# Down products of the feed-forward layers in seven block products, with sums by way of DRAM and the low parts of activation blocks on GpSimd

## The chip, the cores and the metric

The kernel runs on one core of one Trainium2 chip. The metric is the device time of one execution in microseconds; a kernel's time is the median of its runs.

## The reference

One inference step of a one-layer encoder with 1024 prompt tokens and 8 x 16 sample tokens, model width 1024. A feed-forward layer stands at each end of the layer, and both are what matters here (width of the hidden layer 2816):

```python
def swiglu(x, w_gate, w_up, w_down):
    return (jax.nn.silu(x @ w_gate) * (x @ w_up)) @ w_down

x = x + 0.5 * swiglu(rms_norm(x, w['ffn1_norm']), w['ffn1_w_gate'], w['ffn1_w_up'], w['ffn1_w_down'])
# sparse attention and a gated delta rule in parallel, merged, projected and added to x
x = x + 0.5 * swiglu(rms_norm(x, w['ffn2_norm']), w['ffn2_w_gate'], w['ffn2_w_up'], w['ffn2_w_down'])
y = rms_norm(x, final_norm)
```

Everything is float32.

## The kernel before

All 1152 tokens lie in nine tiles of 128 (`x`, one tile to a row of 1024). Each float32 operand of a matrix product is split in a high part, rounded to the type that TensorE takes, and a low part, the rest; `three_passes` (line 151) makes a product as high x high, high x low, low x high. ScalarE writes the high part with a copy, VectorE (in a few places GpSimd) the low part with a subtraction.

`ffn` (line 398) runs twice. Its *gate and up* stage goes over 22 units: unit 2n is the gate weights of a pair n of hidden tiles, unit 2n + 1 the up weights. Six of the nine token tiles are already multiplied there in seven block products, with sums of weight blocks (`take_sum`) and of token blocks; the three plain tiles (`PLAIN`) are multiplied as they are. The items of a unit (`EIGHT`, `SEVEN` in the first four units) pass through a ring of six (`ring`): `keep_item` on ScalarE, `rest_item` on VectorE, `half_item` on TensorE; VectorE folds partial results (`folds`, line 859), ScalarE takes the silu, VectorE the product with the up half (line 850), and SyncE stores the pair's activations to DRAM (`act_d`, line 502).

The *down* stage reads them back by k-tiles: 22 in the second layer, 20 in the first, whose last two are left to the next stage (`Pending`). SyncE loads an activation tile and a weight tile (`load_slot`, lines 512 and 513), two in flight, ScalarE copies the high parts (lines 700 and 702), VectorE makes the low parts (lines 906 and 908), seven slots hold them. `groups` divides the k-tiles in seven groups; for each group TensorE makes all 18 outputs of 128 tokens x 512 columns (`down_proj`, line 1104), three products to a k-tile, and VectorE adds each to `x` (`add_down`, line 920). In the last group of the second layer a tile's final norm follows its two additions (`finish_tile`, line 923; squares on ScalarE, line 580), and SyncE stores it (line 566).

GpSimd makes low parts of the first four items and of the sums of tokens (lines 1004 and 1011) and does nothing more in the layer. Each engine runs its instructions in the order of the code; semaphores order the engines. The profile's tile names carry `ffn_` for both layers.

## Time and profile before

| | us |
|---|---|
| median of 3 runs | 2903.29 |
| lowest, highest | 2898.73, 2906.71 |
| the profiled execution | 2895.88 |
| its span, first to last instruction | 2894.1 |

Busy shares of the span: TensorE 95%, its weight loads 89%, VectorE 60%, ScalarE 35%, GpSimd 15%. The DMA engines moved 247.85 MB. The two feed-forward layers take the first 789 us and the last 830 us or so of the span; what lies between is attention, the delta rule and the merge. In the rows, PE is TensorE, DVE is VectorE, ACT is ScalarE, POOL is GpSimd and SP is SyncE; `SPq` and `POOLq` are DMA issues of these; L840 is line 840. Busy time counts overlapping products once.

### The profile page before, as it was taken

How to read it: one execution, taken by the hardware profiler on the slowest of the kernel's cores; microseconds unless marked ns; L12 is line 12 of the kernel's file. 1: busy time of each engine (PE TensorE's matmuls, PEld its weight loads, DVE VectorE, ACT ScalarE, POOL GpSimd, SP SyncE). 2: the span in 40 equal slices, each digit the busy share in tenths (PEclk: the TensorE clock that was granted, in tenths of full speed). 3: DMA queues.
4: the chain of work that ended last, by engine and by line, in shares of the span. 5: the costliest groups of instructions: out<-in, count | busy, mean ns of one | idle time of the engine just before them, and what ended most of it. 6: DMA issues, size and time to landing. Idle time of an engine off the chain costs nothing. (4 is left out here: it accounts for less than half of the span.)

```text
span 2894.1 us, 41141 instructions
## 1 busy us (share of the span) xinstructions
PE 2747.5 (95%) x15469; PEld 2571.3 (89%) x15469; DVE 1732.8 (60%) x3068; ACT 1001.9 (35%) x1748; POOL 422.4 (15%) x527
## 2 busy tenths in 40 slices
PE   6999999999999999999989769899989999999998
PEld 6999999988889799999978668788789999998887
DVE  6755545655451388899454457678676555556544
ACT  5332232311132444554276425421353223232121
POOL 3000000000010044454130157410020000000000
PEclk9999999999999999999989989999999999999999
DMA  4322122422122022232210323442223212215221
GB/s 161 129 68 77 61 77 77 175 92 87 55 51 44 22 75 74 85 93 92 71 44 12 87 57 81 124 144 93 99 91 122 77 61 77 78 46 205 94 100 66
DMA packets 213725, 247.85 MB, mean 86 GB/s; under 512 B 46393, under 2 KB 180265, under 8 KB 213554
## 3 DMA queue, kind: packets, MB, share of 16 engines
q1 hardware_dynamic: 206402, 217.15, 23.3%
q10 hardware_dynamic: 4752, 18.94, 1.7%
q0 software_dynamic: 2400, 9.44, 0.9%
q8 instruction: 112, 1.84, 0.3%
q14 instruction: 59, 0.48, 0.1%
HBM read 180.29 MB, written 65.14 MB: 85 GB/s over the span
## 5 line engine op out<-in xcount | busy, mean ns | idle before, releaser
L156 PE MATMUL ffn_p<-ffn_slot_d,ffn_slot_a 128*128 128x512 f32 x2268 | 514.5, 389 | 0.0
L156 PEld LDWEIGHTS ffn_p<-ffn_slot_d,ffn_slot_a 128*128 128x128 f32 x2268 | 425.7, 188 | 88.3
L156 PE MATMUL ffn_p<-ffn_plain,ffn_ring 128*128 128x384 f32 x2112 | 396.6, 337 | 5.1 <-DVE ffn_ring L840 5.1
L156 PE MATMUL ffn_p<-ffn_t,ffn_ring 128*128 128x384 f32 x2112 | 386.7, 334 | 0.0
L156 PEld LDWEIGHTS ffn_p<-ffn_plain,ffn_ring 128*128 128x128 f32 x2112 | 371.3, 189 | 6.6 <-DVE ffn_ring L840 6.4
L156 PEld LDWEIGHTS ffn_p<-ffn_t,ffn_ring 128*128 128x128 f32 x2112 | 368.7, 188 | 0.0
L920 DVE SCALAR_TENSOR_TENSOR x<-ffn_p,x 128x512 f32<-128x512 f32 x252 | 173.2, 690 | 238.7 <-PE ffn_p L156 238.7
L156 PE MATMUL ffn_p<-ffn_b,ffn_ring 128*128 128x384 f32 x1584 | 290.2, 335 | 5.2 <-DVE ffn_ring L840 5.2
L156 PEld LDWEIGHTS ffn_p<-ffn_b,ffn_ring 128*128 128x128 f32 x1584 | 276.5, 188 | 5.8 <-DVE ffn_ring L840 5.8
L156 PE MATMUL sp_p_out<-h_hT_hi,sp_w_hi 128*128 128x384 f32 x768 | 258.4, 336 | 0.0
L156 PE MATMUL sp_p_out<-h_hT_hi,sp_w_lo 128*128 128x384 f32 x768 | 257.5, 335 | 0.0
L156 PE MATMUL sp_p_out<-h_hT_lo,sp_w_hi 128*128 128x384 f32 x768 | 257.5, 335 | 0.0
L859 DVE TENSOR_TENSOR ffn_folds<-ffn_p,ffn_folds 128x384 f32<-128x384 f32 x220 | 122.5, 557 | 206.0 <-PE ffn_p L156 205.7
L645 ACT CAST ffn_ring<-ffn_sums 128x512 fp32r<-128x512 f32 x176 | 109.4, 622 | 293.7 <-PE ffn_p L156 274.3
L1682 DVE MAX8 sp_best<-sa_scores 128x8 f32<-128x384 f32 (+3 forms) x201 | 166.1, 866 | 36.0 <-issue 35.1
L1687 DVE MATCH_REPLACE8 sa_scores<-sp_best,sa_scores 128x384 f32<-128x384 f32 (+3 forms) x201 | 170.7, 857 | 0.0
L700 ACT CAST ffn_slot_a<-ffn_raw_a 128x1152 fp32r<-128x1152 f32 x42 | 48.7, 1159 | 325.3 <-DMA ffn_raw_a<-act_d 194.6
L840 DVE TENSOR_TENSOR ffn_ring<-ffn_sums,ffn_ring 128x512 fp32r<-128x512 f32 x176 | 121.1, 689 | 63.3 <-ACT ffn_ring L645 55.7
L156 PEld LDWEIGHTS sp_p_out<-h_hT_hi,sp_w_hi 128*128 128x128 f32 x768 | 145.0, 189 | 0.1
L156 PEld LDWEIGHTS sp_p_out<-h_hT_lo,sp_w_hi 128*128 128x128 f32 x768 | 145.0, 189 | 0.0
L156 PEld LDWEIGHTS sp_p_out<-h_hT_hi,sp_w_lo 128*128 128x128 f32 x768 | 144.9, 189 | 0.0
L645 ACT CAST ffn_ring<-ffn_raw_g 128x512 fp32r<-128x512 f32 x100 | 61.3, 621 | 182.9 <-PE ffn_p L156 182.9
(409 smaller groups left out, 4342.4 us busy)
## 6 DMA issues: line engine op xcount, KB each, us to landing
ffn_raw_g<-in_ffn_w_gate SPq DMA_DIRECT2D x26, 1024.0 KB, 5.4
ffn_raw_u<-in_ffn_w_up SPq DMA_DIRECT2D x26, 1024.0 KB, 5.4
act_d<-ffn_silu SPq DMA_DIRECT2D x22, 1152.0 KB, 4.3
ffn_raw_a<-act_d SPq DMA_DIRECT2D x44, 576.0 KB, 3.9
ffn_raw_d<-in_ffn_w_down SPq DMA_DIRECT2D x44, 512.0 KB, 4.7
h_raw<-in_w_in SPq DMA_DIRECT2D x32, 512.0 KB, 3.9
projected_d<-sp_stage ACTq DMA_DIRECT2D x20, 576.0 KB, 2.8
x<-in_x_prompt SPq DMA_DIRECT2D x16, 512.0 KB, 6.3
```

The costliest lines, as they stand in the source:

```text
L156: mm = nc.tensor.matmul(out, stationary(k)[a], moving(k)[b], start=(start and at == 0 and i == 0), stop=(stop and 3 * at + i == n - 1), sk ...
L645: nc.scalar.copy(m.ring[:, at % RING, 0], m.source(u, item)).then_inc(item_hi, 1)
L700: nc.scalar.copy(a_hi, m.raw_a[:, n % 2]).then_inc(slot_hi, 1)
L840: nc.vector.tensor_tensor(m.ring[:, at % RING, 1], m.source(u, item), m.ring[:, at % RING, 0].bitcast(F32), ALU.subtract).then_inc(item_lo, 1)
L859: nc.vector.tensor_tensor(m.folds[:, out], bank_at[:, 0:TG], m.folds[:, other], ALU.add).then_inc(folded, 1)
L920: nc.vector.scalar_tensor_tensor(out=xs, in0=down_banks[(NO * g + o) % 8][:], scalar=0.5, in1=xs, op0=ALU.mult, op1=ALU.add).then_inc(adde ...
L1682: nc.vector.max(best[:, t, :], row(t))
L1687: nc.vector.match_replace(row(t), best[:, t, :], row(t), TAKEN)
```

## The change

The down products become seven block products as well. Per pair of k-tiles (2kp, 2kp + 1) the activations are a 2 x 2 block matrix of four even token tiles and four odd ones (`EVEN`, `ODD`) against the two k-tiles, and the weights one of the two k-tiles against two column halves. Seven products of block sums (`DOWN`) give the four output blocks; the ninth token tile (`ALONE`) is multiplied with the four weight blocks directly, beside four of the seven products (`BESIDE`). The loop order is turned: all pairs of k-tiles for the first product, then all for the second, and so on; a bank holds a product's sum over k throughout, eight banks in two sides X and Y, and three products are added onto the bank of an earlier one after VectorE has read that (`ONTO`, `READS`).

The sums are made by GpSimd during the gate and up stage: it loads weight blocks by a DMA of its own, makes four sums and writes them to DRAM; when a pair's activations are done it makes four sums of these and writes them to DRAM. In the down stage SyncE loads, step by step, a block or sum of activations and one of weights, four in flight; ScalarE copies the high parts, VectorE makes the weights' low parts and GpSimd the activations'. Eight slots hold activations and fourteen hold weights. ScalarE waits for GpSimd's sums of two pairs earlier before it writes new silus over these activations. The final norms go in the order odd tiles, the single tile, even tiles.

```diff
-SLOTS = 7
+A_SLOTS, W_SLOTS, RAWS = 8, 14, 4
+PLACES = SIDE_A + PLAIN + SIDE_B
+EVEN, ODD, ALONE = PLACES[:4], PLACES[5:], PLACES[4]
-SLOT_STEPS = {"S2": 0, "S3": 1, "A22": 2}
+AHEAD = {"A11": 0, "S2": 1, "S3": 2, "A12": 3, "S1": 4, "A22": 5}
+DOWN = (("P1", "A11", "B11", "X"), ("P6", "S2", "T2", "Y"), ("P2", "A12", "B21", "X"), ("P7", "S3", "T3", "Y"),
+        ("P5", "S1", "T1", "X"), ("P4", "A22", "T4", "Y"), ("P3", "S4", "B22", "X"))
+ONTO = ("P2", "P4", "P3")
+BESIDE = {"P1": ("B11", 0, 0), "P2": ("B21", 1, 0), "P7": ("B12", 0, 1), "P3": ("B22", 1, 1)}
+READS = {"P1": ((0, 1), (1, 0), (1, 1)), "P6": ((0, 1), (1, 0), (1, 1)), "P2": ((0, 0),), "P7": ((1, 1),),
+         "P5": ((1, 1),), "P4": ((1, 0),), "P3": ((0, 1),)}
...
-        sizes = (2, 3, 3, 3, 4, 3, 4) if finish else (2, 3, 3, 3, 3, 3, 3)
+        NP = NM if finish else NM - 1
+        steps = [(product, kp) for product in range(len(DOWN)) for kp in range(NP)]
...
+            def load_step(at):
...
+                if at == 0:
+                    sp.wait_ge(turned, 2 * NT)
+                    sp.wait_ge(h_sum_lo, 4 * PAIRS)
+                    sp.wait_ge(t_out, 16 * NP)
+                if at >= RAWS:
+                    sp.wait_ge(a_lo, at - RAWS + 1)
...
+                    if j >= RAWS:
+                        sp.wait_ge(w_lo, j - RAWS + 1)
+                    sp.dma_start(m.raw_w[:, j % RAWS], weights_source(used_in[j][1], kp)).then_inc(raw_w_in[j % RAWS], 16)
...
                     if n >= 2:
                         act_stored(act, n - 2)
+                        act.wait_ge(act_summed, 4 * (n - 1))
...
+            def keep_step(at):
+                if at < A_SLOTS:
+                    first_use(act, at)
+                else:
+                    step_over(act, at - A_SLOTS)
+                width = 640 if DOWN[steps[at][0]][0] in BESIDE else 512
+                act.wait_ge(raw_a_in[at % RAWS], 16 * raws_before[at])
+                nc.scalar.copy(m.slot_a[at % A_SLOTS][:, 0, 0:width], m.raw_a[:, at % RAWS, 0:width]).then_inc(a_hi, 1)
...
+            for at, (product, kp) in enumerate(steps):
+                if at:
+                    rest_step(at + A_SLOTS - 1)
...
+                if finish and at in range(6 * NP + 5, 6 * NP + 9):
+                    finish_tile(at - 6 * NP - 5)
+                if kp == NP - 1:
+                    for key in reads:
+                        if key[0] == DOWN[product][0]:
+                            read(key)
+                            if finish and key[0] == "P3" and key[1] != "alone":
+                                finish_tile(key[1] + 4)
             if finish:
-                finish_tile(NT - 1)
+                finish_tile(8)
...
+            def sum_acts(n):
...
+                nc.gpsimd.tensor_tensor(out[:, 0], block(1, 0), block(1, 1), ALU.add).then_inc(act_summed, 1)
+                nc.gpsimd.tensor_tensor(out[:, 2], block(0, 0), block(1, 0), ALU.subtract).then_inc(act_summed, 1)
+                pool.wait_ge(act_summed, 4 * n + 1)
+                nc.gpsimd.tensor_tensor(out[:, 1], out[:, 0], block(0, 0), ALU.subtract).then_inc(act_summed, 1)
+                pool.wait_ge(act_summed, 4 * n + 3)
+                pool.dma_start(act_sums_d[n, 0:3].rearrange("i p c -> p i c"), out[:]).then_inc(act_sum_out, 16)
+                pool.wait_ge(act_sum_out, 32 * n + 16)
+                nc.gpsimd.tensor_tensor(out[:, 0], block(0, 1), out[:, 1], ALU.subtract).then_inc(act_summed, 1)
+                pool.wait_ge(act_summed, 4 * n + 4)
+                pool.dma_start(act_sums_d[n, 3], out[:, 0]).then_inc(act_sum_out, 16)
+
+            def rest_acts(at):
+
+                width, slot = 640 if DOWN[steps[at][0]][0] in BESIDE else 512, m.slot_a[at % A_SLOTS]
+                pool.wait_ge(a_hi, at + 1)
+                nc.gpsimd.tensor_tensor(slot[:, 1, 0:width], m.raw_a[:, at % RAWS, 0:width], slot[:, 0, 0:width].bitcast(F32),
+                                        ALU.subtract).then_inc(a_lo, 1)
...
+            for n in range(NP):
+                sum_blocks(n)
+                if n + 1 < NP:
+                    load_blocks(n + 1)
+                if n == NM - 1:
+                    for at in range(len(AHEAD)):
+                        rest_acts(at)
+                sum_acts(n)
+            for at in range(len(AHEAD) if NP == NM else 0, len(steps)):
+                rest_acts(at)
...
+            def down_step(at):
...
+                order = list(range(4))
+                if name in BESIDE:
+                    order = ["alone"] + order if last else order + ["alone"]
+                for pair in order:
+                    if pair == "alone":
+                        mm = onto_bank(pair, down_banks["XY"[side == "X"]][3], slice(512, 640),
+                                       m.slot_w[weights_of[at][-1] % W_SLOTS], False)
+                    else:
+                        mm = onto_bank(pair, down_banks[side][pair], slice(pair * P, (pair + 1) * P), w, name in ONTO)
...
-            for g in range(len(groups)):
-                for o in range(NO):
-                    down_proj(g, o)
+            for at in range(len(steps)):
+                down_step(at)
```

## Rows read from the trace of the kernel before

**Rows 1.** The page's slices, TensorE: busy tenths in 40 equal slices
```profile
PE   6999999999999999999989769899989999999998
```

**Rows 2.** Chain of waits in order of time: start us, length us, what
```profile
2146.21 739.71 PE ffn_p L156 x3900
...
2885.94 0.69 DVE x L920
```

**Rows 3.** Table by stage: stretch, its us, busy us (instructions) by engine, clock, DMA share, GB/s
```profile
2146.00:2200.00 54.00, 53.79 (x310) 53.79 (x311) 41.75 (x71) 23.16 (x42) 0.00 (x0) 1.00 0.31 100
...
2250.00:2350.00 100.00, 100.00 (x578) 100.00 (x578) 52.35 (x86) 28.94 (x52) 0.00 (x0) 1.00 0.24 80
...
540.00:600.00 60.00, 60.00 (x271) 50.31 (x270) 38.99 (x50) 13.27 (x12) 0.00 (x0) 1.00 0.50 188
```

**Rows 4.** Timeline where the down stages begin and the first ends: start us, us, instruction
```profile
543.76 16.52 PE L156 MATMUL ffn_p<-ffn_slot_d,ffn_slot_a 128*128 128x512 f32 x72
...
788.80 0.69 DVE L920 SCALAR_TENSOR_TENSOR x<-ffn_p,x 128x512 f32<-128x512 f32 x1 [1.35 <-PE ffn_p L156]
...
2616.42 23.78 PE L156 MATMUL ffn_p<-ffn_slot_d,ffn_slot_a 128*128 128x512 f32 x104
```

**Rows 5.** By tile, down slots: duration ns min/median/max, first and last start
```profile
L156 PE MATMUL ffn_p<-ffn_slot_d,ffn_slot_a x2268: 387/389/398, 543.8 to 2885.5; 128*128 128x512 f32 x189
```

**Rows 6.** Timeline of the merge stage, TensorE: products of three-product runs
```profile
1990.05 0.39 PE L156 MATMUL mg_p_out<-o_c_hi,o_t_hi 128*128 128x512 f32 x1
...
1990.72 0.39 PE L156 MATMUL mg_p_out<-o_c_hi,o_t_hi 128*128 128x512 f32 x1
```

**Rows 7.** The page's costliest groups, ScalarE casts: count | busy us, mean ns | idle
```profile
L645 ACT CAST ffn_ring<-ffn_sums 128x512 fp32r<-128x512 f32 x176 | 109.4, 622 | 293.7 <-PE ffn_p L156 274.3
...
L700 ACT CAST ffn_slot_a<-ffn_raw_a 128x1152 fp32r<-128x1152 f32 x42 | 48.7, 1159 | 325.3 <-DMA ffn_raw_a<-act_d 194.6
```

**Rows 8.** By line, GpSimd: duration ns min/median/max, first and last start
```profile
L1011 POOL TENSOR_TENSOR ffn_t<-ffn_sums_of_h,ffn_t x24: 1262/1506/2278, 29.5 to 2137.8; 128x512 fp32r<-128x512 f32 x24
...
L1643 POOL TENSOR_TENSOR sp_w_lo<-h_raw,sp_w_hi x32: 2348/2402/2419, 1019.9 to 1419.1; 128x1024 fp32r<-128x1024 f32 x32
...
L3175 POOL DMA_DIRECT2D mg_gate_a<-projected_d x7: 527/528/551, 1892.6 to 2009.5; - x7
```

**Rows 9.** By line, VectorE, 2092 to 2145 us, its waiters, and 2300 to 2400 us
```profile
L840 DVE TENSOR_TENSOR ffn_ring<-ffn_raw_u,ffn_ring x8: 685/986/1782, 2106.0 to 2138.3; 128x512 fp32r<-128x512 f32 x8
...
  PE ffn_p L156: 2.5, 2
...
L790 DVE TENSOR_TENSOR ffn_b<-ffn_p,ffn_b x9: 680/681/692, 2100.3 to 2132.5; 128x512 fp32r<-128x512 f32 x9
...
L840 DVE TENSOR_TENSOR ffn_ring<-ffn_sums,ffn_ring x17: 684/692/693, 2303.2 to 2394.7; 128x512 fp32r<-128x512 f32 x17
```

**Rows 10.** DMA issues: count, KB, median us to landing; and one issue of SyncE
```profile
ffn_raw_d<-in_ffn_w_down SPq DMA_DIRECT2D x44, 512.0 KB, 4.7
...
x<-in_x_prompt SPq DMA_DIRECT2D x16, 512.0 KB, 6.3
...
mg_gate_b<-projected_d POOLq DMA_DIRECT2D x7, 576.0 KB, 5.9
...
2658.91 0.43 SPq L513 DMA_DIRECT2D ffn_raw_d<-in_ffn_w_down  x1
```

**Rows 11.** Timeline, VectorE: the last products of the last two pairs
```profile
2571.45 0.56 DVE L850 TENSOR_TENSOR ffn_silu<-ffn_silu,ffn_folds 128x384 f32<-128x384 f32 x1
...
2617.21 0.56 DVE L850 TENSOR_TENSOR ffn_silu<-ffn_silu,ffn_folds 128x384 f32<-128x384 f32 x1
```

**Rows 12.** Timeline of the end: norm of the last tile, its store
```profile
2888.36 0.15 DVE L758 TENSOR_SCALAR ffn_mean<-ffn_sumsq 128x1 f32<-128x1 f32 x1
...
2888.98 1.28 DVE L929 SCALAR_TENSOR_TENSOR x<-x,ffn_rstd,ffn_last_gain_b 128x1024 f32<-128x1024 f32 x1
...
2890.29 0.33 SPq L566 DMA_DIRECT2D out_y_sample<-x  x1
```

More of the change, by code:

```diff
@@ L432, in ffn @@
         FIRST = first_of[0, True]
-        x_order = tuple((len(items) + j) % RING for j in range(RING)) + (8, 6, 7)
         by_pool = 4
@@ L446, in nth_of, with step_over, first_use @@
                                                2 * n + {2: 1, 5: 2}[nth])
-        sizes = (2, 3, 3, 3, 4, 3, 4) if finish else (2, 3, 3, 3, 3, 3, 3)
-        n_slots = sum(sizes)
-        groups = [range(sum(sizes[:g]), sum(sizes[:g + 1])) for g in range(len(sizes))]
-        group_of = {n: g for g, group in enumerate(groups) for n in group}
+        act_sums_d, w_sums_d = sums_d
+        last_order = ODD + (ALONE,) + EVEN
+        NP = NM if finish else NM - 1
+        steps = [(product, kp) for product in range(len(DOWN)) for kp in range(NP)]
+        weights_of, used_in, raws_before = [], [], [0] * len(steps)
+        for at, (product, kp) in enumerate(steps):
+            name = DOWN[product][0]
+            weights_of.append([len(used_in) + i for i in range(2 if name == "P7" else 1)])
+            used_in += [(at, name_w, kp) for name_w in ((DOWN[product][2],) + (("B12",) if name == "P7" else ()))]
+            here = 2 if name in ("P7", "P3") else 1
+            raws_before[at] = (raws_before[at - RAWS] if at >= RAWS else 0) + here
+        reads, nth_read, nth_banked = [], {}, {}
+        for product, (name, _, _, _) in enumerate(DOWN):
+            order = [(name, "alone")] if name in BESIDE else []
+            for key in order + [(name, pair) for pair in range(4)]:
+                nth_banked[key] = len(nth_banked) + 1
+            for key in order + [(name, pair) for pair in ((3, 0, 1, 2) if name == "P6" else range(4))]:
+                reads.append(key)
+        count = 0
+        for key in reads:
+            count += 1 if key[1] == "alone" else len(READS[key[0]])
+            nth_read[key] = count
+        def step_over(eng, at):
+            product, kp = steps[at]
+            if kp == NP - 1:
+                eng.wait_ge(banked, nth_banked[DOWN[product][0], 3])
+            else:
+                eng.wait_ge(step_done, at - product + 1)
+        def first_use(eng, j):
+            if FREED_BY[j] == 0:
+                eng.wait_ge(h_sum_lo, 4 * PAIRS)
+                lo_ready(eng, position[LAST - 1, "S4", True])
+            else:
+                eng.wait_ge(item_done, position[LAST, EIGHT[FREED_BY[j] - 1], True] + 1)
         def act_stored(eng, n):
@@ new lines, in _, with add_to @@
+            last_add, adds = {}, []
+            def add_to(t, half, bank):
+                if (t, half) in last_add:
+                    dve.wait_ge(added, last_add[t, half])
+                else:
+                    dve.wait_ge(x_back[t], 16)
+                xs = x[:, t, half * 512:half * 512 + 512]
+                nc.vector.scalar_tensor_tensor(out=xs, in0=bank[:], scalar=0.5, in1=xs, op0=ALU.mult,
+                                               op1=ALU.add).then_inc(added, 1)
+                adds.append(t)
+                last_add[t, half] = len(adds)
@@ new lines, in read, with finish_tile @@
+            def read(key):
+                name, pair = key
+                side = {n: x_or_y for n, _, _, x_or_y in DOWN}[name]
+                dve.wait_ge(banked, nth_banked[key])
+                if pair == "alone":
+                    add_to(ALONE, BESIDE[name][2], down_banks["XY"[side == "X"]][3])
+                else:
+                    for odd, half in READS[name]:
+                        add_to((EVEN, ODD)[odd][pair], half, down_banks[side][pair])
+            def finish_tile(nth):
+                t = last_order[nth]
+                take_mean(t, nth)
+                invert(t, nth)
+                if nth == 0:
@@ new lines, in sum_acts, with block @@
+            def sum_acts(n):
+                act, out = m.silu[n % 2], m.act_sums
+                def block(token, k):
+                    return act[:, k].rearrange("p g t -> p (g t)")[:, token * 640:token * 640 + 512]
+                if n < 2:
+                    pool.wait_ge(prod_done, 4 * n + 8)
+                else:
+                    pool.wait_ge(prod_done, nth_of(n, 6))
+                if n:
+                    pool.wait_ge(act_sum_out, 32 * n)
+                nc.gpsimd.tensor_tensor(out[:, 0], block(1, 0), block(1, 1), ALU.add).then_inc(act_summed, 1)
[8 more added lines that the diff above has]
+                pool.dma_start(act_sums_d[n, 3], out[:, 0]).then_inc(act_sum_out, 16)
@@ L3325, in encoder_step @@
     act_d = nc.dram_tensor("act_d", (NF, P, TOK), F32, kind="Internal").ap()
+    sums_d = [nc.dram_tensor(n, (NF // 2, 4, P, 512), F32, kind="Internal").ap() for n in ("act_sums_d", "w_sums_d")]
     x_d = nc.dram_tensor("x_d", (NT, P, D), F32, kind="Internal").ap()
```

292 lines of the change are left out of this document (173 added, 119 removed).

## The prediction

> **What bounds the kernel now.** I read the busy slices first: TensorE is at 9 tenths in nearly every slice in which a feed-forward layer runs [rows 1]. Then the chain of waits, followed back from the end: from 2146.21 us to 2885.92 us it is TensorE alone, 739.7 us without a step to another engine [rows 2]. The table by stage confirms it from the other side: TensorE is busy for the whole of a stretch of the gate and up stage and of the down stage, while VectorE stands at 52% and 65%, ScalarE at 29% and 22%, and GpSimd at nothing; the clock is granted in full [rows 3]. So time falls here only if TensorE gets less to do, and falls by all of that as long as nobody else becomes late.
>
> The two down stages: the first runs from 543.76 us to the last addition's start at 788.80 us, 245.0 us for 20 k-tiles x 18 outputs x 3 passes = 1080 products; the second from 2616.42 us to 2885.92 us, 269.5 us for 22 x 18 x 3 = 1188 [rows 2, 4]. Both give 0.2269 us for a product of 512 columns, without gaps; the 2268 in the trace are these two sums [rows 5].
>
> **The change, part by part.** *TensorE.* Two k-tiles used to cost 2 x 18 x 3 = 108 products. Now seven block products on four pairs of token tiles and four products for the tile that stands alone make (7 x 4 + 4) x 3 = 96. With 10 and 11 pairs of k-tiles that is 960 and 1056 instead of 1080 and 1188: 252 fewer, and 252 x 0.2269 = **57.2 us less**. A new thing is that a bank gets three products and then the next bank follows. In the merge stage this order exists already: from the first product of one output to the first of the next is 0.67 us, 0.22 us each [rows 6]. So I take the old pace.
>
> *ScalarE* copies per pair of k-tiles four activation blocks of 640, three of 512 and eight weight blocks of 512. 512 take 622 ns, 1152 take 1159 ns [rows 7], hence some 0.73 us for 640: 4 x 0.73 + 11 x 0.62 = 9.8 us. TensorE needs 96 x 0.2269 = 21.8 us for them. Hidden.
>
> *GpSimd and VectorE in the down stage.* VectorE loses the low parts of the activations and 126 - 48 = 78 of its additions a layer. It has the low parts of eight weight blocks: 8 x 0.69 = 5.5 us. GpSimd gets the activations' low parts. Its 512-wide subtraction takes 1.26 us at least and 2.28 us at most, a 1024-wide one 2.40 us [rows 8]; that makes 640 about 1.6 us, and 4 x 1.6 + 3 x 1.3 = 10.3 us. The spread between 1.26 and 2.28 has a cause that the rows show: where GpSimd worked beside it, the VectorE subtraction with both inputs in SBUF took up to 1782 ns, against at most 693 ns in a quiet stretch; one with an input in PSUM stayed at 692 ns or below [rows 9]. So the two delay each other on SBUF inputs. Even one after the other, 10.3 + 5.5 = 15.8 us fits in 21.8. Hidden, the 48 additions too, as they read PSUM.
>
> The Trainium skill, in SBUF — State Buffer, "Who interferes with whom", says that a VectorE instruction with two SBUF inputs and a GpSimd instruction that reads SBUF block each other entirely. That agrees with which rows grew. By it alone the 15.8 us would stand and so would the sum.
>
> *The raw ring.* Only four steps are in flight: SyncE may load step n when step n - 4 has its low part. One round is two issues of 0.43, a landing of 4.7 to 6.3 us, a copy of 0.73 and a low part of 1.6 to 2.8 [rows 7, 8, 10], so 7.9 to 10.7 us, and four steps of TensorE take 4 x 12 x 0.2269 = 10.9 us or more. I take the lower end, as the existing slot loads are of this kind, and eight slots give a lead of seven steps. In bytes: 2 MB of activations and 2 MB of weights in 21.8 us are 193 GB/s; a stretch with 188 GB/s had the engines half busy [rows 3]. Hidden.
>
> *Gate and up.* Here GpSimd gets, per two units, four block sums of the weights, four of the activations and three DMAs, and ScalarE's silu waits for the sums of two pairs earlier. From the pair's last product on [rows 11], a sum of activations takes 3 x 1.5 + 0.53 + 5.9 + 1.5 = 12.4 us [rows 8, 10], and the wait comes due a whole pair and a half unit later (132 products of 0.173 us make a unit of 22.8 us, 578 of them in 100 us [rows 3], so over 50 us). The wait costs nothing. The collision on SBUF inputs remains: at most 8 x (1.78 - 0.69) = 8.7 us of VectorE's time per pair of units, which is 45.7 us long and in which VectorE is idle for 48%. Only in the first four units, without the plain tiles, is VectorE busy 41.75 of 54 us [rows 3]; there a delay can reach TensorE. From 0 to 8 us for both layers; I take **3 us**.
>
> *The hand-over to the second down stage.* Weight sums are written once 12.4 + 4 x 1.5 + 0.5 + 5.9 us have gone by after the product at 2571.45 us [rows 11], at about 2597 us; then the first loads, copies and low parts, ready by some 2604 us, ahead of 2616.42. But GpSimd does six low parts, and then the last sums of activations, which wait for the product that ends at 2617.77 us [rows 11]: 12.4 us, a DMA issue and the seventh low part end near 2632.5. Six steps last TensorE 6 x 15 x 0.2269 = 20.4 us, until 2636.8. About 4 us are left. I cost it at nothing, with 10 us as the other end. In the first layer the last pair is left out, and GpSimd is done with the sums long before.
>
> *The end.* Before, a tile came out every 24 products or 5.4 us, and only the last one's norm was bare: 8.2 us from the last product to the end [rows 2, 12]. Now the last step gives five tiles within 15 x 0.2269 = 3.4 us. VectorE needs for each an addition of 0.69 (0.61 to its successor) and mean, root, reciprocal and scaling, 1.90 from 2888.36 to 2890.26 [rows 12]. Its first addition starts 2.7 us ahead of TensorE's end; in program order (alone, one addition, norm, addition, norm, ...) the last scaling ends about 10.1 us after it, instead of 4.3. **5.7 us more** (5 to 7). In the first layer the last five additions keep pace with the banks (0.69 against 0.68).
>
> Sum: - 57.2 + 5.7 + 3 = **- 48.5 us**. The profiled execution took 2895.88 us (span 2894.1), so 2847.4; the median of the three runs, 2903.29, is 0.26% above it, and the same ratio of 0.9833 on it gives **2855 us**.
>
> **The rivals.** *Collision through the whole gate and up stage* (the one that is slower). Place: the folds and ring parts of VectorE that TensorE waits for; price: up to 8.7 us per pair of units, of which TensorE's six-deep ring and the folds' leads hide the rest. The gain is gone when each of the 21 pairs loses 48.5 / 21 = 2.3 us; if half the 8.7 us shows, the time is 2855 + 21 x 4.3 = 2945. For it: TensorE did wait for ring parts around 2092 to 2145 us, just where the long subtractions stand [rows 9]. Against it: VectorE is idle almost half of the time later, and the sums fall into four short bursts. The mutual exclusion of the Trainium skill's SBUF page would make this rival's price the full one, 1.26 us or so per GpSimd instruction; the longest row, 1.09 us over, is near that.
>
> *The raw ring as the pace.* If landing grows to 9 us under twice the bytes, a round is 12.8 us or 3.2 us a step, over 147 steps 470 us against TensorE's 457: about 2870. Break-even is 508.9 us (the old 514.5 less the longer end), 3.46 a step, a landing of about 10 us, beyond any row of this kind.
>
> *The late hand-over.* If GpSimd's instructions run at their longest at the start of the second down stage, TensorE waits there for 3 to 12 us: about 2865.
>
> *No fewer products in time.* Products on three-product runs at a worse pace would take the gain itself; 12% slower would cancel it. The merge rows exclude it.
>
> **How the numbers follow.** Forecast with its own bounds (stalls of 0 to 8 us, 2846 to 2863): 0.62. Better, with a shorter end or none of the stalls (2838 to 2846): 0.05. Late hand-over or partial collision (2863 to 2880): 0.16. Ring as the pace (2865 to 2900): 0.08, most of it still faster. Collision throughout: 0.09, of which 0.07 slower than before. The range of 2840 to 2882 holds about 0.85. 0.3% is what a measurement can tell from no change: faster (below 2894.6) 0.88, same 0.05, slower (above 2912.0) 0.07.
>
> **What would show it.** Right: products in the down stages fall to 2016 at 0.227 us with no waits between; the two down stages last about 218 and 240 us; the chain is again TensorE from the gate stage to the end, and then about 14 us of VectorE and the store. Wrong: TensorE waits named by a ring part, a fold or a slot's low part from GpSimd; VectorE's SBUF subtractions above 1 us throughout the gate and up stage with TensorE gaps behind them; ScalarE waiting for raw blocks in most steps.

## The result, and the profile after

The changed kernel takes 2875.74 us (median of 4 runs, 2872.14 to 2877.42), the kernel before 2901.15 us beside it (median of 4): a ratio of 0.9908, 95% interval 0.9889 to 0.9927. The time is inside the forecast's range, and 20.7 us above the forecast of 2855. It lies in the case that the prediction called late hand-over or partial collision (2863 to 2880). The profiled execution took 2877.42 us, so profile against profile the gain is 18.5 us where 48.5 was worked out. This ledger shows where the rest is. Each column runs from the start of one stage's first product to the start of the next stage's (a down stage to the end of its last product, the end to the end of the span). All are read from the timelines of TensorE.

| us | start to first down stage | first down stage | from there to gate and up of the second layer | its gate and up | second down stage | end | span |
|---|---|---|---|---|---|---|---|
| before | 543.76 | 245.00 | 1357.45 | 470.21 | 269.49 | 8.19 | 2894.1 |
| after | 546.21 | 226.19 | 1362.67 | 473.11 | 252.89 | 14.53 | 2875.6 |
| difference | +2.45 | -18.81 | +5.22 | +2.90 | -16.60 | +6.34 | -18.5 |
| predicted | +1.5 | -27.2 | 0 | +1.5 | -29.9 | +5.7 | -48.5 |

(The 3 us foreseen for both gate and up stages stand half in each.)

So 21.7 of the missing 30 us are in the two down stages, 5.2 in the stretch between the layers, which the change doesn't touch, and the rest in two terms that were a little small.

The chain of waits of the changed kernel, in order of time (start us, length us, what), answers [rows 2]. Before, it was TensorE alone for 739.7 us, up to its last product.

```profile
2148.42 459.93 PE ffn_p L156 x2652
...
2613.69 8.96 DMA act_sums_d<-ffn_act_sums
2622.73 1.30 POOL ffn_act_sums L1160
2624.32 5.63 DMA act_sums_d<-ffn_act_sums
2633.21 1.38 SPq L591
2635.00 7.48 DMA ffn_raw_a<-act_sums_d
2645.24 8.15 DVE ffn_slot_w L993 x5
...
2655.86 68.27 PE ffn_p L156 x288
2725.41 3.08 DVE x L1009 x5
2728.54 129.82 PE ffn_p L156 x570
```

TensorE is still the whole chain until 2608 us. Then the chain leaves it for 47 us: the store of GpSimd's last sums, SyncE, a load from those sums, five low parts of weights on VectorE, the bank reads (L1009). TensorE works through most of these 47 us on steps that are ready and waits for 7.8 of them. The waits of TensorE in the two down stages (total us, times, longest us), first stage, then second:

```profile
PE ffn_p L156 <- DVE x L1009: 5.5, 3, 3.0
...
PE ffn_p L156 <- DVE x L1009: 8.6, 2, 7.2
PE ffn_p L156 <- DVE ffn_slot_w L993: 0.6, 1, 0.6
```

They add up to 14.7 us, nearly all for a bank that VectorE has not read. The timeline of the second down stage shows the longest of them (start us, us, instruction):

```profile
2608.18 34.20 PE L156 MATMUL ffn_p<-ffn_slot_w,ffn_slot_a 128*128 128x512 f32 x150
2642.97 5.68 PE L156 MATMUL ffn_p<-ffn_slot_w,ffn_slot_a 128*128 128x512 f32 x24 [0.60 <-DVE ffn_slot_w L993]
2655.86 71.26 PE L156 MATMUL ffn_p<-ffn_slot_w,ffn_slot_a 128*128 128x512 f32 x300 [7.20 <-DVE x L1009]
```

And VectorE's timeline at the same place:

```profile
2643.89 11.32 DVE L993 TENSOR_TENSOR ffn_slot_w<-ffn_raw_w,ffn_slot_w 128x512 fp32r<-128x512 f32 x7 [1.06 <-ACT ffn_slot_w L779]
2655.13 7.25 DVE L1009 SCALAR_TENSOR_TENSOR x<-ffn_p,x 128x512 f32<-128x512 f32 x12
```

The lone tile's bank of P1 is complete about 2643.7 us (estimated: one output of 0.68 us into the 11th step, which starts at 2642.97). VectorE reads it at 2655.13, because in its program the low parts up to seven steps ahead stand before the reads, and seven of them came late and in a heap, 11.32 us of them.

The table by stage (columns as in [rows 3]): two stretches of the gate and up stage, then the first down stage up to its wait and behind it, then the second from before its wait on.

```profile
2300.00:2400.00 100.00, 100.00 (x578) 100.00 (x578) 63.37 (x86) 30.40 (x55) 35.00 (x31) 1.00 0.39 135
2150.00:2200.00 50.00, 50.00 (x291) 50.00 (x290) 40.05 (x61) 18.84 (x33) 16.67 (x14) 1.00 0.52 181
...
546.00:582.00 36.00, 36.00 (x161) 29.84 (x160) 15.54 (x12) 13.45 (x22) 15.01 (x10) 1.00 0.93 341
...
586.00:593.00 7.00, 7.00 (x25) 5.55 (x24) 7.00 (x13) 2.28 (x4) 2.59 (x2) 0.76 0.38 137
...
2616.00:2648.00 32.00, 31.40 (x139) 25.74 (x138) 11.96 (x8) 11.45 (x19) 14.36 (x11) 1.00 0.91 337
2648.00:2656.00 8.00, 0.80 (x4) 0.34 (x3) 8.00 (x7) 4.79 (x8) 8.00 (x5) 0.71 0.93 298
2656.00:2660.00 4.00, 4.00 (x10) 3.13 (x11) 4.00 (x8) 1.14 (x2) 1.62 (x2) 0.50 0.80 263
2660.00:2665.00 5.00, 5.00 (x20) 4.01 (x19) 5.00 (x7) 1.15 (x3) 1.79 (x1) 0.84 0.06 14
2665.00:2720.00 55.00, 55.00 (x244) 45.55 (x243) 38.40 (x37) 25.65 (x42) 28.31 (x18) 1.00 0.70 221
```

Two things stand out. At the start of each down stage the DMA engines are 91 to 93% busy with 337 to 341 GB/s, against 50% and 188 GB/s in [rows 3]. And behind a stop TensorE is slow for a while: 0.50 of its clock, the 1.2 GHz level, from 2656 to 2660 us, 0.84 on average in the five behind, then full. The 101 products from 585.47 us took 24.65 us up to the issue of the next one where 22.92 would do, the 300 from 2655.86 took 71.10 for 68.07: together 4.8 us more on top of the waits.

By tile, the down slots (ns min/median/max, first and last start) answer [rows 5] and [rows 9]:

```profile
L156 PE MATMUL ffn_p<-ffn_slot_w,ffn_slot_a x2016: 387/389/794, 546.2 to 2860.7; 128*128 128x512 f32 x184
...
L993 DVE TENSOR_TENSOR ffn_slot_w<-ffn_raw_w,ffn_slot_w x168: 672/1368/3386, 529.9 to 2835.2; 128x512 fp32r<-128x512 f32 x168
```

The 2016 products are there; the longest of 794 ns are those at half clock. VectorE's low parts, costed at 0.69 us each, have a median of 1.37.

### The profile page after: what moved, and what is told of

Its sections match the earlier page's. It is cut to its first block and busy times, and to the rows that moved or that the text cites. A ratio compares the mean times of both kernels' runs of the same rounds, so it can differ in the third digit from the quotient of the medians.

```text
span 2875.6 us, 41915 instructions
## 1 busy us (share of the span) xinstructions
PE 2703.6 (94%) x15217; PEld 2530.5 (88%) x15217; DVE 1819.6 (63%) x2996; ACT 1100.3 (38%) x1979; POOL 943.6 (33%) x926
## 5 line engine op out<-in xcount | busy, mean ns | idle before, releaser
L156 PE MATMUL ffn_p<-ffn_slot_w,ffn_slot_a 128*128 128x512 f32 x2016 | 464.3, 392 | 14.7 <-DVE x L1009 14.1
L156 PEld LDWEIGHTS ffn_p<-ffn_slot_w,ffn_slot_a 128*128 128x128 f32 x2016 | 380.7, 189 | 97.9 <-DVE x L1009 17.5
L993 DVE TENSOR_TENSOR ffn_slot_w<-ffn_raw_w,ffn_slot_w 128x512 fp32r<-128x512 f32 x168 | 215.2, 1298 | 171.7 <-ACT ffn_slot_w L779 171.6
L1168 POOL TENSOR_TENSOR ffn_slot_a<-ffn_raw_a,ffn_slot_a 128x640 fp32r<-128x640 f32 (+1 forms) x147 | 226.1, 1544 | 236.6 <-ACT ffn_slot_a L772 236.2
L926 DVE TENSOR_TENSOR ffn_ring<-ffn_sums,ffn_ring 128x512 fp32r<-128x512 f32 x176 | 177.1, 1009 | 50.7 <-ACT ffn_ring L718 43.7
L772 ACT CAST ffn_slot_a<-ffn_raw_a 128x640 fp32r<-128x640 f32 (+1 forms) x147 | 100.5, 683 | 238.8 <-PE ffn_p L156 170.8
L1153 POOL TENSOR_TENSOR ffn_act_sums<-ffn_silu 128x512 f32<-128x512 f32 x21 | 34.6, 1646 | 476.6 <-DVE ffn_silu L936 476.6
```

The costliest lines, as they stand in the source:

```text
L156: mm = nc.tensor.matmul(out, stationary(k)[a], moving(k)[b], start=(start and at == 0 and i == 0), stop=(stop and 3 * at + i == n - 1), sk ...
L772: nc.scalar.copy(m.slot_a[at % A_SLOTS][:, 0, 0:width], m.raw_a[:, at % RAWS, 0:width]).then_inc(a_hi, 1)
L926: nc.vector.tensor_tensor(m.ring[:, at % RING, 1], m.source(u, item), m.ring[:, at % RING, 0].bitcast(F32), ALU.subtract).then_inc(item_lo, 1)
L993: nc.vector.tensor_tensor(slot[:, 1], m.raw_w[:, j % RAWS], slot[:, 0].bitcast(F32), ALU.subtract).then_inc(w_lo, 1)
L1153: nc.gpsimd.tensor_tensor(out[:, 0], block(1, 0), block(1, 1), ALU.add).then_inc(act_summed, 1)
L1168: nc.gpsimd.tensor_tensor(slot[:, 1, 0:width], m.raw_a[:, at % RAWS, 0:width], slot[:, 0, 0:width].bitcast(F32), ALU.subtract).then_inc(a_ ...
```

## The experiments

Two theories were set against each other. **A, order and lateness**: the steps of a down stage come late at its start, and VectorE, which works in program order, does the late low parts before it reads the banks that TensorE waits for. **B, collision**: the low parts on GpSimd make those on VectorE slow, and that alone makes the reads late. The waits given below are the profiled executions' own. The kernel before ran beside each group: 2898.36 us (the first four), 2897.4 (the second four), 2898.2 (the last).

**Order of the load of x.** SyncE loads x back, two tiles each behind the loads of steps 6 to 10; before the tiles 6, 7 and 8 it waits for the store of GpSimd's last sums, whose memory these tiles overwrite. With the old order that wait stands behind the loads of step 8; here the tiles 7, 6 and 8 come last, and it stands behind those of step 9.

```
-            tiles = [ALONE] + [t for pair in zip(EVEN, ODD) for t in pair]
+            tiles = [ALONE, EVEN[0], ODD[0], EVEN[1], ODD[1], EVEN[3], EVEN[2], ODD[2], ODD[3]]
```

> The changed kernel with one edit: of the nine tiles of x that SyncE loads back during the first product, the three that lie over GpSimd's buffer of sums (7, 6, 8) come last, so that SyncE meets its wait for the last sums three loads later; still two tiles a step. Theory A (the missing gain went into the hand-over at the start of the down stages, where the reload of x and this wait starve the steps and VectorE, which works in program order, reads the banks late): the 13.5 us in which SyncE stands in the second layer go, TensorE's wait of 7.2 us there falls to about the 3.0 us of the first layer, which had the burst and no such wait; 4 to 6 us off the changed kernel, some 2870 us. Rival B (VectorE is late because its subtractions collide with GpSimd's, 1.30 us a piece for 0.69): nothing moves, 2876 us.

Measured: 2873.47 us, ratio 0.991 (0.9888 to 0.9933), so the same as the change within the interval. The long wait of the second down stage fell from 7.2 to 5.3 us, SyncE's own wait for the sums from 12.7 to 10.4 us. The second down stage fell from 252.89 to 249.54 us. Theory A had foreseen 2870 us and a wait of 3.0: the place was right, but moving SyncE's wait by one step does not take it away.

**x one tile a step.** The same, and one tile a step instead of two (`tiles[:2]` becomes `tiles[:1]`).

> As e1_x_order, and one tile of x a step for nine steps in place of two a step for five. Theory A: the waits of 3.0, 0.6 and 7.2 us behind the first product go, and with them the stretches at a lower granted clock that follow them (2.1 and 3.2 us); the two waits of 1.4 us and the one of 1.1 us at later product ends stay. 13 to 16 us off the changed kernel: about 2861 us, the down stages near 220 and 242 us. Rival B: collisions go on as before, and at most 3 us are gained.

Measured: 2874.18 us, ratio 0.9906 (0.9887 to 0.9925). This is not the 2861 us that theory A had foreseen. SyncE's wait for the sums is gone from its list, and the waits of TensorE are 4.2 us in the first down stage (5.5 before the edit) and 5.3 in the second (9.2), the longest 1.7 and 3.9. The down stages are 3.1 and 4.2 us shorter. In the first one VectorE's low parts now come one every 2.6 us or so, but the reads still stand behind what has come. The burst of x and SyncE's wait are a part of the lost time and not the whole.

**Bank reads first.** At the end of a block product VectorE reads the banks and only then does the next low part.

```
-                if at:
+                if at and kp < NP - 1:
                     rest_step(at + A_SLOTS - 1)
...
                             if finish and key[0] == "P3" and key[1] != "alone":
                                 finish_tile(key[1] + 4)
+                    rest_step(at + A_SLOTS - 1)
```

> The changed kernel with one edit on VectorE: at the end of a product the banks are read before the low part of the step seven ahead, not after it. That low part can come only when ScalarE's copy has a slot, and the slot comes free when TensorE is through the step before the last. Theory A: the three small waits of TensorE (1.4, 1.1 and 1.4 us) go; the two long ones stay, since there six earlier low parts are late too, and shorten by 1 to 2 us: 4 to 6 us off, some 2871 us. Rival B: a wait at a product's end is the collision's, so it shrinks by less than 1 us in all.

Measured: 2870.29 us, ratio 0.989 (0.9868 to 0.9913). The first down stage fell from 226.19 to 220.07 us, the second from 252.89 to 248.11; of the small waits at later products the two of 1.43 us are gone and that of 1.06 us is 0.46. What is left is in this timeline of VectorE, second down stage:

```profile
2641.93 9.65 DVE L993 TENSOR_TENSOR ffn_slot_w<-ffn_raw_w,ffn_slot_w 128x512 fp32r<-128x512 f32 x6 [1.05 <-ACT ffn_slot_w L779]
2651.50 7.85 DVE L1009 SCALAR_TENSOR_TENSOR x<-ffn_p,x 128x512 f32<-128x512 f32 x13
```

One low part fewer in front of the reads, six still there. So part of the order is shown to be a cause, and the rest of it is the lead.

**GpSimd's sums narrow.** In the gate and up stage GpSimd's sums are 16 columns wide instead of 512; as many DMAs as before write blocks in place of sums, so the down stages work on other numbers.

```
-                nc.gpsimd.tensor_tensor(t[:, 0], b[:, 0, 1], b[:, 0, 0], ALU.subtract).then_inc(t_summed, 1)
...
+                    nc.gpsimd.tensor_tensor(t[:, i, 0:16], b[:, 0, 1, 0:16], b[:, 0, 0, 0:16], ALU.subtract).then_inc(t_summed, 1)
```

> The changed kernel with GpSimd's sums in the gate and up stage 16 columns wide instead of 512; what is written to DRAM comes straight from the blocks, with the same DMAs in number and nearly in bytes, so the sums that the down stage reads are wrong. It leaves out the work of the sums alone. Theory: the gate and up stages were longer by 2.5 us (first layer, from the start) and 2.9 us (second) because GpSimd's sums collide with VectorE's ring parts and sums in the first units; both go back to 543.8 and 470.2 us, 5 us off, the down stages unchanged: some 2871 us. Rival: the added DMAs are the cause, then both stay at 546.2 and 473.1 us.

Measured: 2871.12 us, ratio 0.991 (0.9885 to 0.9935). The second gate and up stage took 471.78 us, between 470.21 before and 473.11 with the change, and the first layer up to its down stage 543.80, which is the 543.76 of before (with full sums that stretch took 545.6 to 549.2 us in eleven profiles). VectorE's ring parts from the sums went back to a mean of 702 ns from 1009. So the collision in gate and up exists and costs a few us, as the 3 us term said. The waits of the first down stage stayed (5.5 us). Those of the second fell from 9.2 to 5.6, and the stage to 247.97 us: without the chain of full sums the stores of the last pair leave early, and SyncE waits for them 0.6 us instead of 12.7, with the burst of x as it was.

**Low parts on VectorE.** The other end of theory B: GpSimd does nothing in a down stage.

```
+                width, act_slot = 640 if DOWN[steps[at][0]][0] in BESIDE else 512, m.slot_a[at % A_SLOTS]
+                dve.wait_ge(a_hi, at + 1)
+                nc.vector.tensor_tensor(act_slot[:, 1, 0:width], m.raw_a[:, at % RAWS, 0:width],
+                                        act_slot[:, 0, 0:width].bitcast(F32), ALU.subtract).then_inc(a_lo, 1)
                 for j in weights_of[at]:
...
```

> The low parts of the activation blocks (147 in the two down stages) go from GpSimd to VectorE; GpSimd keeps its sums. Theory A (the lost time is the hand-over into the down stages: late steps, and VectorE in program order): VectorE's two subtractions of a step take 0.69 and about 0.78 us when nothing runs beside them, together 1.5 us a step, against about 1.3 us on average for its one beside GpSimd, so the lead grows no faster; waits of TensorE in the down stages stay within 3 us of the changed kernel's 5.5 and 7.2 us, and the time is 2873 to 2880 us. Theory B (the collision of GpSimd and VectorE is what makes the reads late): with it gone the steps come early, both long waits and the slow stretches behind them vanish, and the time is 2858 to 2866 us.

Measured: 2871.26 us, ratio 0.9899 (0.9877 to 0.9921); neither theory's time, but between them. Groups of VectorE by line (busy us, mean ns | idle before):

```profile
L997 DVE TENSOR_TENSOR ffn_slot_w<-ffn_raw_w,ffn_slot_w 128x512 fp32r<-128x512 f32 x168 | 113.7, 685 | 18.2 <-ACT ffn_slot_w L779 18.0
...
L992 DVE TENSOR_TENSOR ffn_slot_a<-ffn_raw_a,ffn_slot_a 128x640 fp32r<-128x640 f32 x84 | 69.7, 830 | 88.4 <-ACT ffn_slot_a L772 88.4
...
L992 DVE TENSOR_TENSOR ffn_slot_a<-ffn_raw_a,ffn_slot_a 128x512 fp32r<-128x512 f32 x63 | 43.4, 689 | 56.5 <-ACT ffn_slot_a L772 56.5
```

And the weights' low parts of the changed kernel, beside GpSimd's:

```profile
L993 DVE TENSOR_TENSOR ffn_slot_w<-ffn_raw_w,ffn_slot_w 128x512 fp32r<-128x512 f32 x168 | 215.2, 1298 | 171.7 <-ACT ffn_slot_w L779 171.6
```

All 315 low parts took VectorE 226.8 us alone, where 168 of them took 215.2 us beside GpSimd's 147. The waits: 1.9 us in the first down stage instead of 5.5, and 6.7 in the second instead of 9.2, the longest still 5.3. The down stages fell to 220.66 and 248.58 us, by nearly as much as with the reads first, so theory B holds a part of the truth. Collision makes a heap of late low parts longer; it isn't what puts the heap in front of the reads.

**Lead of five.** Bank reads first, and VectorE's low parts run five steps ahead, not seven (the edit is shown on top of that of *Bank reads first*).

```
-            for at in range(len(AHEAD), A_SLOTS):
+            for at in range(len(AHEAD), 6):
...
-                    rest_step(at + A_SLOTS - 1)
+                    rest_step(at + 5)
```

> On VectorE the bank reads at the end of a block product stand before the next low part, as in e3_read_first, and its low parts of the weights run five steps ahead instead of seven, so that a read has two late low parts fewer in front of it. Theory A (program order on VectorE): the waits that e3_read_first kept (1.2 us in the first down stage, 5.5 us in the second) fall to under 1 us and under 2 us, the down stages to 218 to 220 and 240 to 244 us, and the time to 2860 to 2867 us. Theory B (collision): the reads are late because each subtraction is slow, and a shorter lead makes the steps later by as much; the second stage stays at 247 to 250 us and the time at 2868 to 2873 us. A lead of five could be too short: then TensorE waits on ffn_slot_w in the middle of the stages.

Measured: 2861.62 us, ratio 0.9869 (0.9844 to 0.9895). The first down stage takes 217.81 us without a wait, which is 960 x 0.2269; the second takes 244.53. The time is theory A's forecast; the waits left in the second stage, 2.8 us, and its length are a little above what theory A gave (under 2 us, 240 to 244). The collision goes on: VectorE's low parts of weights have a mean of 1143 ns here, 1298 in the changed kernel, against 685 with GpSimd idle. No wait on a slot appeared behind the 11th step of a stage. In the second:

```profile
PE ffn_p L156 <- DVE x L1009: 2.1, 1, 2.1
PE ffn_p L156 <- DVE ffn_slot_w L993: 0.7, 1, 0.7
```

**What keeps the second hand-over.** Two edits on top of the lead of five. The first lets GpSimd do its low parts of steps 6 to 8 between its last two sums, the place that the prediction had suspected:

```
+                if n == NM - 1:
+                    for at in range(len(AHEAD), len(AHEAD) + 3):
+                        rest_acts(at)
                 pool.wait_ge(act_sum_out, 32 * n + 16)
...
```

> e8_lead5 with one thing more: GpSimd does its low parts of steps 6 to 8 of the second layer between its last two sums instead of behind both. e8_lead5 kept 2.1 + 0.7 us of waits and some 2 us of slow clock in the second down stage (244.5 us against 239.6 us of products). If the late low part of step 6 on GpSimd is their cause, the second down stage falls to 239.5 to 241 us and the time to 2856 to 2860 us; if SyncE's burst of x and its wait for the sums are, it stays at 243 to 246 us and 2859 to 2864 us. The first down stage has no such sums in front of it and stays at 217.8 us.

Measured: 2865.11 us, ratio 0.9887 (0.987 to 0.9903); the second down stage is longer, 248.95 us, above both forecasts.

```profile
PE ffn_p L156 <- DVE ffn_slot_w L993: 3.3, 1, 3.3
PE ffn_p L156 <- DVE x L1009: 2.2, 1, 2.2
...
SPq L591 <- DMA act_sums_d<-ffn_act_sums: 17.6, 1, 17.6
```

The third line says why (SyncE's waits, same kernel): the last sum is stored later, and SyncE, in program order ahead of a tile of x, waits 17.6 us for it (12.7 without this edit), with the loads of the next steps behind it. GpSimd's low part of step 6 begins 8.4 us behind the stage's first product here, 16.8 without the edit, and the stage is longer all the same.

The second edit is the load of x in the other order and one tile a step:

> e8_lead5 with one thing more: x is loaded back one tile a step, the tiles that wait for GpSimd's last sum at the end. If the burst of x and SyncE's wait behind it cause what e8_lead5 kept in the second down stage (2.1 + 0.7 us of waits, some 2 us of slow clock), that stage falls to 239.5 to 241 us and the time to 2856 to 2860 us; if the late low part of step 6 on GpSimd does, it stays at 243 to 246 us and 2859 to 2864 us. The first down stage stays at 217.8 us.

Measured: 2857.64 us, ratio 0.9866 (0.985 to 0.9883). TensorE in the second down stage, to the edge of the window shown:

```profile
2599.81 100.58 PE L156 MATMUL ffn_p<-ffn_slot_w,ffn_slot_a 128*128 128x512 f32 x443
```

Both down stages are without a wait, 217.80 and 239.56 us, 57.1 us less than before. SyncE's wait for the sums is gone from its list, and VectorE's low parts still have a mean of 1149 ns. GpSimd's late low part of step 6, left where it was, costs nothing. In the second layer it takes both edits: with x alone mended 5.3 us of waits were left, with VectorE's order alone 2.8, with both none. This edit thins the burst of x and takes SyncE's wait away at once. The run with narrow sums took the wait alone and left 5.6 us of TensorE's waits, x one tile a step took both and left 5.3, each with VectorE's old order. So of the two it is SyncE, in order behind the sums' store, that counts in the second layer, with VectorE's order behind it; the burst alone adds little there.

**The end, tile by tile.** On the unaltered change, the last five steps of the last block product are done pair by pair (the lone tile, then 0, 1, 2, 3) instead of step by step.

```
+                for pair in ("alone", 0, 1, 2, 3):
...
+                    for at in range(len(steps) - n_last, len(steps)):
```

> The last five steps of the second layer's last block product are done pair by pair (the lone tile first, then pairs 0, 1, 2, 3) instead of step by step, so that the last tiles come complete some 3.4 us apart and not 0.7 us. If the longer end is the chain of tiles on VectorE (2.4 us a tile for four tiles that come together), the stretch from TensorE's last product to the end falls from 14.5 us to about 8.5 us and the time by 5 to 6 us, to 2868 to 2872 us. If the end is bound by something that every version of it has (the last store's landing, ScalarE's square and root), it stays at 14 us and the time at 2873 to 2878 us. Waits in the down stages should be those of the changed kernel.

Measured: 2874.9 us, ratio 0.991 (0.9889 to 0.9931). In its profile the end falls from 14.53 to 8.76 us, as expected, and nothing else of the ledger moves by more than 2.2 us. The median misses the 2868 to 2872 us expected: the 5.8 us don't show in it, and its interval reaches some 6 us either way. The additions of the last tiles, VectorE:

```profile
2852.27 0.69 DVE L1009 SCALAR_TENSOR_TENSOR x<-ffn_p,x 128x512 f32<-128x512 f32 x1 [2.71 <-PE ffn_p L156]
...
2859.07 0.69 DVE L1009 SCALAR_TENSOR_TENSOR x<-ffn_p,x 128x512 f32<-128x512 f32 x1 [0.90 <-PE ffn_p L156]
...
2862.47 0.69 DVE L1009 SCALAR_TENSOR_TENSOR x<-ffn_p,x 128x512 f32<-128x512 f32 x1 [0.90 <-PE ffn_p L156]
```

They come 3.4 us apart and VectorE waits for TensorE in front of each. In the changed kernel they stood 2.4 us apart with VectorE itself the limit:

```profile
2862.12 0.68 DVE L1009 SCALAR_TENSOR_TENSOR x<-ffn_p,x 128x512 f32<-128x512 f32 x1
...
2864.53 0.68 DVE L1009 SCALAR_TENSOR_TENSOR x<-ffn_p,x 128x512 f32<-128x512 f32 x1
...
2869.97 1.28 DVE L1032 SCALAR_TENSOR_TENSOR x<-x,ffn_rstd,ffn_last_gain_b 128x1024 f32<-128x1024 f32 x1
```

**All together.** Reads first, lead of five, x one tile a step, the split sums and the end by tiles.

> All together: x reloaded one tile a step, bank reads before low parts, a lead of five, GpSimd's low parts of steps 6 to 8 of the second layer between its last two sums, and the last five steps of the last product pair by pair. By theory A the waits at the two hand-overs go (down stages 218 to 220 and 240 to 243 us) and the end falls from 14.5 to about 8.5 us: 2852 to 2860 us. By theory B the second down stage stays at 247 us or more, and the time at 2862 to 2867 us.

Measured: 2852.49 us (2850.48 to 2859.89), ratio 0.9838 (0.9813 to 0.9863): faster than both kernels. Its chain is again what it was before the change:

```profile
2137.74 709.38 PE ffn_p L156 x3756
...
2848.36 1.28 DVE x L1032
```

Down stages 217.80 and 239.56 us, end 8.70. Beside x one tile a step the split sums cost nothing here (SyncE's wait for the store is 6.9 us and hides), and they gain nothing that shows either.

**Both kernels once more**, for the stretch between the layers.

> The kernel before, once more, for a second profile. Between the first down stage and the second layer's gate and up products, code that the change does not touch took 1357.5 us in its first profile and 1362 to 1370 us in ten profiles of the changed kernel and its variants. If that is the scatter between executions, this profile shows 1360 to 1368 us there and a span of 2896 to 2905 us; if the change itself slows that code, it shows 1356 to 1359 us again.

> The changed kernel, once more, for a second profile. The waits of TensorE in the down stages should come back in the same places (5.5 us in the first, 7 to 9 us in the second, as theory A has them, since they come from the order of work and not from an accident of one execution); the stretch between the layers, 1362.7 us in the first profile, should stand within 5 us of that of e12_before_again.

Measured: 2896.2 and 2876.26 us. TensorE's waits in the down stages of the changed kernel came back to the tenth (5.5 us; 8.6 us, the longest 7.2), so they belong to the order of work. The stretch between the layers was 1357.60 us before and 1360.63 after. My expectation of scatter was wrong on the side of before: it repeated its 1357.45, while the changed kernel and its variants lie between 1360.6 and 1370.4 in twelve profiles. Within the stretch the attention is longer (178.9 us in both profiles of before, 182.8 and 182.0 in the two of after), and the scores ahead of it by 0.4 and 2.5 us; TensorE's waits there are on the same things. But the attention isn't the whole of it: with the lead of five it takes 178.9 us again, and the stretch 1363.9. TensorE makes the same 7513 products there in all fourteen profiles. Why they take 3 to 13 us more, these runs don't show. It stays open.

## Why the prediction was right and wrong

The time lies in the range, but not by the working that gave the forecast: 21.7 of the 30 us missing in the profile stand in the down stages, where the sum had nothing against the gain. The case that it met, late hand-over, had named GpSimd's instructions as the cause and the second down stage as the place. The waits there, 9.2 us, are inside its 3 to 12, and the rest of the distance came from elsewhere. That the range held is in part luck.

**TensorE, 57.2 us less: right as a price, wrong as a saving.** The products are 2016, and where nobody stops TensorE they run at the old pace: 960 in 217.80 us, 0.2269 each, in the first down stage of the run with the lead of five. With order and loads mended, the two down stages fall by 27.2 + 29.9 = 57.1 us. As the change stands, 35.4 of these come through; 14.7 are waits, 4.8 the slow clock behind the two longest, and the other 2.2 us lie at the edges of the stops and behind the shorter ones.

**ScalarE: right.** No step of TensorE waits for it. Blocks of 640 and 512 take a mean of 730 and 622 ns, the 0.73 and 0.62 assumed (the sum of a pair is 9.7 us and not 9.8).

**GpSimd and VectorE in the down stage: right in size, and it hid the failing step.** GpSimd's low parts take 1658 ns (640 columns) and 1392 (512) on the average, the assumed 1.6 and 1.3. Of a VectorE low part the prediction said that one after the other would still fit, and they do: 8 x 1.30 = 10.4 us of 21.8. But "the 48 additions too, as they read PSUM" counted them as durations only. **This is the step that failed**: an addition frees a bank, and its place in VectorE's order is behind low parts for up to seven steps ahead. The lead of seven steps, put down in *the raw ring* as a safety, is what stood in front of the reads. Reads first and a lead of five give the first down stage its full 217.8 us, with VectorE's low parts still at a mean of 1143 ns.

**The raw ring: the round was right in the middle, wrong at the start.** The down stages' loads land in a median of 3.2 to 3.4 us, less than the 4.7 to 6.3 taken. But at the start of a stage x comes back in the same queue, and the DMA engines are over 90% busy; then the loads of the second down stage land in 7.5 us (activations) and 10.7 us (weights), as the issues from 2608 to 2650 us show (count, KB, median us to landing):

```profile
x<-x_d SPq DMA_DIRECT2D x9, 512.0 KB, 7.8
...
ffn_raw_a<-act_d SPq DMA_DIRECT2D x5, 320.0 KB, 7.5
ffn_raw_w<-in_ffn_w_down SPq DMA_DIRECT2D x5, 256.0 KB, 10.7
```

The prediction took its bytes from an average of 193 GB/s and overlooked the nine tiles of x, 512 KB each, that come back within five steps. It had a rival with this place and a landing of 10 us as break-even, but for a whole stage, not for its first ten steps.

**Gate and up, 3 us: a little small.** 2.45 + 2.90 in the ledger; with narrow sums 0.04 + 1.57. The mechanism is the one named. Of the 1.57 left, 1.03 is that the stage's first twelve products took 3.40 us instead of 2.37, behind a stop of 2.58 us that the kernel before has there too. The collision throughout, the slower rival, did not come: behind the first product of the second layer's gate and up TensorE waits 1.1 us in all (2.7 in the second profile of the changed kernel), and none of it later than 14 us into the stage, although VectorE's ring parts from sums rose to a mean of 1009 ns [rows 9]: VectorE at 63 of 100 us had room for it.

**The hand-over, at nothing with 10 us as the other end: the place was right, the mechanism not.** GpSimd's seventh low part was in time: the last four sums and two stores began at 2609.61 and the part was done by 2626.5 (half of the row 2624.93 shown in the last section), two us before TensorE would need it, six steps or 20.4 us behind 2608.18. What was late is what stands behind the sums' store on another queue:

```profile
2613.69 0.77 POOL L1158 DMA_DIRECT2D act_sums_d<-ffn_act_sums  x1 [0.30 <-POOL ffn_act_sums L1156]
2622.73 1.29 POOL L1160 TENSOR_TENSOR ffn_act_sums<-ffn_silu,ffn_act_sums 128x512 f32<-128x512 f32 x1 [8.27 <-DMA act_sums_d<-ffn_act_sums]
...
2616.81 13.48 SPq L591 DMA_DIRECT2D x<-x_d  x2
2630.39 0.38 SPq L575 DMA_DIRECT2D ffn_raw_a<-act_d  x1
```

SyncE stands before tile 7 of x, and with it the loads of step 9 and all later ones, for 12.7 of the 13.48 us of that row, until the second of the two stores has landed. The first, which the last sum waits for, took 8.96 us instead of the 5.9 of [rows 10], the second 5.63. The prediction followed GpSimd's queue and not SyncE's. That the first layer has no such hand-over was wrong too: it has the burst of x, and lost 8.4 us. Of its 5.5 us of waits x one tile a step takes 1.3; the rest goes with VectorE's order.

**The end, 5.7 us: right.** 6.3 measured, the same chain of additions and norms; the 2.4 us a tile are what VectorE's order makes, and giving TensorE's last outputs out one tile at a time takes 5.8 us of it back.

**Not in the sum:** the stretch between the layers, 5.2 us in the first profile, 3.0 in the second.

## What to carry to other kernels

An instruction that frees something for the bottleneck is judged by what stands before it in its engine's order, not by its own duration: look-ahead work put in front of it is harmless while it is early and delays it in full when it comes late. At the start of a stage follow every in-order queue, the loading one too, through its waits for other engines, with the landings of that stretch and not of the flow. And when a gain stays out, compare the stage with its own floor (products times the pace): here that showed at once that 21.7 us were waits and their echo, and where to look.

## What the runs showed of the hardware

A short stop of TensorE can be paid for twice. In the changed kernel the granted clock behind the stop of 7.2 us was 0.50 for four us and 0.84 for the next five, the products up to 794 ns instead of 389, and 1.7 and 3.0 us were lost behind the two longest stops. The loss doesn't follow the length of the stop: in the run with the other order of x the clock was 1.00 from 585.25 to 590 us, directly behind a stop of 2.9 us, and the 273 products there took 62.47 us (64.08 behind the changed kernel's 3.0); in the run with x one tile a step it was 0.50 for four us behind a stop of 3.9, and some 3.1 us were lost. In the run with the lead of five and x spread, without a stop, no product of the down stages exceeded 398 ns.

VectorE can wait out more than one GpSimd instruction, as the timelines of GpSimd and VectorE of the changed kernel have it:

```profile
2624.93 3.09 POOL L1168 TENSOR_TENSOR ffn_slot_a<-ffn_raw_a,ffn_slot_a 128x640 fp32r<-128x640 f32 x2
...
2625.19 3.39 DVE L993 TENSOR_TENSOR ffn_slot_w<-ffn_raw_w,ffn_slot_w 128x512 fp32r<-128x512 f32 x1 [6.83 <-ACT ffn_slot_w L779]
```

The one low part took 3.39 us beside two of GpSimd and ended 0.56 us behind them; with GpSimd idle it takes 0.69. The Trainium skill, SBUF — State Buffer, "Who interferes with whom", has the two block each other entirely. These rows agree with that. What GpSimd takes over is then worth little: the work of both engines took VectorE alone only 5% longer than its own share took beside GpSimd (226.8 against 215.2 us).
